# Where the two halves of the weights begin in a partition: 192 and 64 modulo 256 in place of 128

## The reference, cut to what matters

```
h = rms_norm(x, norm_mix_w);  z = h @ w_in + b_in            # 1024 x 5640
mixed = sigmoid(..) * (ya @ w_proj_att) + sigmoid(..) * (yb @ w_proj_mlstm)
x = x + mixed @ w_out
h2 = rms_norm(x, norm_mlp_w)
x = x + square(relu(h2 @ w_ff1)) @ w_ff2                     # 1024 x 4096, 4096 x 1024
```

## Time and profile before

| | |
|---|---|
| time, median of 3 runs | 2530.49 us (2530.07 to 2531.1) |
| profiled execution: its time, its span | 2530.58 us, 2528.8 us |
| PE busy | 2458.0 us, 97% of the span |
| PEld busy | 1994.5 us, 79% |
| POOL, DVE, ACT busy | 1098.9, 991.2, 870.1 us |
| DMA | 215.18 MB, 85 GB/s on average |
| granted TensorE clock | 0.991 on average |

### The profile page before, as it was taken

The page is one execution under the profiler, slowest core; times in us unless marked ns, Lnnn a source line. Parts: engine busy times, 40 slices in busy tenths (PEclk is TensorE's granted clock), DMA queues, the critical chain, the costliest instruction groups (busy, mean ns, idle before and its releaser), DMA issues.

```text
span 2528.8 us, 30042 instructions
## 1 busy us (share of the span) xinstructions
PE 2458.0 (97%) x11732; PEld 1994.5 (79%) x11732; DVE 991.2 (39%) x1582; ACT 870.1 (34%) x1093; POOL 1098.9 (43%) x808
## 2 busy tenths in 40 slices
PE   8899999999999999899999999999999999999998
PEld 6767788888888867688888888798776688888887
DVE  4545564310212354564320212557585534322202
ACT  4255333331323345333431323442234323322213
POOL 4332345554544422335554554342343245555543
PEclk9999999999999999999999999999999999999999
DMA  4221223223322221223222322231122133223221
GB/s 138 84 67 51 67 84 100 86 98 100 100 100 88 84 67 51 79 71 100 83 100 100 100 99 69 84 92 51 52 88 67 55 100 100 89 93 100 100 100 67
DMA packets 174028, 215.18 MB, mean 85 GB/s; under 512 B 7652, under 2 KB 155044, under 8 KB 173924
## 3 DMA queue, kind: packets, MB, share of 16 engines
q1 hardware_dynamic: 171572, 210.39, 25.9%
q10 hardware_dynamic: 2352, 3.31, 0.4%
HBM read 211.20 MB, written 2.10 MB: 84 GB/s over the span
## 4 chain that ended last, share of the span: by engine, by line
issue 49%; POOL 30%; PE 19%; DMA 0%; POOLq 0%; DVE 0%; ACT 0%; SPq 0%
POOL w_lo L290 30%; PE ps L331 3%; PE ps L330 3%; PE ps L329 3%; PE ps L736 3%; PE ps L1755 2%; PE ps L1753 2%; PE ps L1757 2%; DMA w_raw<-in_w_in 0%; POOLq L301 0%; PE ps L322 0%; PE ps L355 0%; PE ps L349 0%; PE ps L348 0%; PE ps L319 0%
## 5 line engine op out<-in xcount | busy, mean ns | idle before, releaser
L290 POOL TENSOR_TENSOR w_lo<-w_raw,w_hi 128x512 fp32r<-128x512 f32 x804 | 1098.7, 1399 | 1403.2 <-ACT w_hi L276 1391.2
L276 ACT ACTIVATE w_hi<-w_raw 128x2048 fp32r<-128x2048 f32 x200 | 382.9, 1915 | 1033.0 <-PE ps L331 394.0
L736 PE MATMUL ps<-h_hi,w_hi 128*128 128x512 f32 (+1 forms) x936 | 393.8, 421 | 15.1 <-POOL w_lo L290 12.9
L736 PE MATMUL ps<-h_hi,w_lo 128*128 128x512 f32 (+1 forms) x936 | 369.0, 394 | 0.0
L736 PE MATMUL ps<-h_lo,w_hi 128*128 128x512 f32 (+1 forms) x936 | 368.5, 394 | 0.0
L329 PE MATMUL ps<-h_hi,w_hi 128*128 128x512 f32 x816 | 319.0, 391 | 0.0
L331 PE MATMUL ps<-h_hi,w_lo 128*128 128x512 f32 x816 | 317.5, 389 | 0.0
L330 PE MATMUL ps<-h_lo,w_hi 128*128 128x512 f32 x816 | 317.4, 389 | 0.0
L736 PEld LDWEIGHTS ps<-h_hi,w_hi 128*128 128x128 f32 (+1 forms) x936 | 175.8, 188 | 76.2 <-issue 23.1
L736 PEld LDWEIGHTS ps<-h_lo,w_hi 128*128 128x128 f32 (+1 forms) x936 | 175.6, 188 | 43.1 <-issue 7.5
L736 PEld LDWEIGHTS ps<-h_hi,w_lo 128*128 128x128 f32 (+1 forms) x936 | 175.2, 187 | 41.4
(11 more groups left out here) (408 smaller groups left out, 3665.6 us busy)
## 6 DMA issues: line engine op xcount, KB each, us to landing
w_raw<-in_w_in SPq DMA_DIRECT2D x72, 1024.0 KB, 5.2
w_raw<-in_w_ff SPq DMA_DIRECT2D x64, 1024.0 KB, 5.2
w_raw<-in_w_ffn_in SPq DMA_DIRECT2D x22, 1024.0 KB, 5.1
w_raw<-in_w_out SPq DMA_DIRECT2D x12, 1024.0 KB, 5.1
w_raw<-in_w_ffn_out SPq DMA_DIRECT2D x11, 1024.0 KB, 4.9
w_raw<-in_w_proj_att SPq DMA_DIRECT2D x4, 1024.0 KB, 5.0
w_raw<-in_w_proj_mlstm SPq DMA_DIRECT2D x4, 1024.0 KB, 5.1
w_raw<-in_w_up_ssd SPq DMA_DIRECT2D x4, 1024.0 KB, 5.3
```

Source lines behind the costliest of these rows:

```text
L276: act.activation(k.whi[:, slot * SLOT:(slot + 1) * SLOT], k.wraw[:, slot * SLOT:(slot + 1) * SLOT], ACT.Copy).then_inc(k.hi_done, CHUNKS)
L290: pool.tensor_tensor(k.wlo[:, a:a + T], k.wraw[:, a:a + T], k.whi[:, a:a + T], ALU.subtract)\
L736: mm = pe.matmul(out, lhs, rhs, start=i == 0 and n == 0, stop=stop and n == 2)
```

## The change

The bytes at which tensors begin are moved. `w_hi` lies 64 bytes further up, at 192 modulo 256. Another 128 bytes are left free ahead of `w_lo`, which so lies 192 bytes further up, at 64 modulo 256, and all that is placed behind it (`xT`, `w_raw`, `constants`, `cos`, `sin` and the small ones) moves up by 192 bytes as well. `h_hi`, `h_lo` and the arena stay where they are. Every engine has the same instructions in the same order as before.

```diff
         k.arena, k.arena_words = (k.top + 127) // 128 * 128, ARENA
         k.top = k.arena + 4 * ARENA
-        k.whi, k.wlo = k.keep("w_hi", 2 * SLOT, F32R), k.keep("w_lo", 2 * SLOT, F32R)
+        k.top += 64
+        k.whi = k.keep("w_hi", 2 * SLOT, F32R)
+        k.top += 128
+        k.wlo = k.keep("w_lo", 2 * SLOT, F32R)
         k.xT = k.keep("xT", KD * T)
         k.wraw = k.keep("w_raw", 2 * SLOT)
```

## The result

The changed kernel takes 2565.65 us (median of 4 runs, 2565.2 to 2566.81), the kernel before, run beside it, 2530.28 us (median of 4, 2529.84 to 2531.1). The ratio is **1.014, with a 95% interval of 1.0123 to 1.0158**: 35.4 us slower. I had predicted 2530.5 us, no change that can be told. The prediction was wrong, and the time lies outside its range (2506 to 2550) as well.

The account below looks back on a forecast made before the run. The prediction took the kernel as bound by how fast PE can start matmuls (226.7 ns each). All terms were 0, so the profiled 2530.58 us, 0.1 us above the median, gave 2530.5 us; range 2506 to 2550 us.

Parts of the forecast that it names:

- Loaded pieces move against the stream: 8952 matmuls loading weights beside streamed tokens: moved load starts cost 0 us, bounds -119 to +49 us.
- Seven of the eight possible offsets, one spacing: Job loading 8 columns, stepping 32 bytes per tile: triples claimed at 0.69, 0.695 and 0.693 us whatever the load's start.
- the readings meet more: Slower rival, loads and streams on PE: 2550 or 2569 us; chance 0.06 from 2550 us, 0.08 for 2536 to 2550.
- the narrow jobs: Jobs loading only 8 or 16 columns on PE: 0.693 us a triple, claimed unchanged wherever the load starts.
- The rule weighed in the prediction: PE's separate SBUF read ports: loading the next tile takes nothing from the running matmul, so the change is worth 0 us.
- ACT and POOL at other offsets: ACT and POOL access `w_raw`, `w_hi`, `w_lo` at new offsets: 0 us; +6 or -6 us if POOL changed 10%.
- DMAs further up: Weight loads landing 192 bytes further up: 0 us, hidden, 5.2 us in a unit of 10.9.
- The streamed weights: 1248 matmuls in which weights stream, from moved starts: 0 us, bounds +-17 us.
- the extra: 13.3 ns per reduced-float32 matmul at full clock, above one column per tick (213.3 ns for 512 columns).
- The bound of +49 us: Upper bound for 8952 moved loads on PE: stream never settles, +5.5 ns each.
- faster: Rival: load and stream readings part; 2395 us if wholly (chance 0.07), 2506 to 2525 us in part (0.11).

Follow-up runs that it names:

- e1_behind: Only what lies behind `w_hi` and `w_lo` moved 192 bytes further up against the kernel before: 2530.81 us, ratio 1.0003.
- e3_all64: Weights, streamed activations and arena all moved 64 bytes further up against the kernel before: 2529.85 us, ratio 1.0002.
- e13_alone: Kernel before plus an appended stage of matmuls, PE alone, start of load minus start of stream chosen per line: 226.7 ns at 0, 233.3 at 64 bytes.
- e11_both224: Both `w_hi` and `w_lo` moved 224 bytes further up against the kernel before: 2576.7 us, ratio 1.018.
- the alternations: Lines of e13_alone in which two pairs of load and stream starts alternate: 228.5, 230.0, 232.1 and 233.3 ns.

## Why the prediction was wrong, step by step

**The step that failed** is "Loaded pieces move against the stream", which I costed at "0 ns x 8952 = 0 us". It measured +5.2 ns in the settled stretches (226.6 to 231.8) and +39.2 us over the 8715 matmuls that pay it. Nothing else of the change costs: e1_behind, with the weights at their old places and only what lies behind them moved, is at 1.0003, and e3_all64, where weights and streams move together, at 1.0002. Two thoughts led to the 0, and both are wrong:

- From the earlier trace rows, 8 and 16 columns at one spacing whatever their start, I concluded for all loads. They speak for narrow loads alone. And the earlier trace rows left out the triple ahead of them, the only one of the job at distance 0, which took 0.68 us in place of 0.693: the sentence "Seven of the eight possible offsets, one spacing" stood on six offsets that were timed, and the two that were missing held the one that differs. e13_alone shows both side by side: 8 columns 231.0 and 231.8 ns at distance 0 and 64, 128 columns 226.7 and 233.3.
- "A load of 128 columns passes over 512 bytes, twice around 256, and would meet every slice whatever its start." Its start matters all the same, 226.7 against 233.3 ns. It passes every slice, but at a time that its start sets against the stream; the loads with wider steps, which lose the 226.7 at distance 0, speak for that, though no run shows the two readings in time. The load of one word is at 229.2, 231.8 and 231.8; so the wide load doesn't only disturb. At distance 0 it helps by 2.5 ns against a load of one word and 4.3 against one of 8 columns, at 64 it costs 1.5.

The sentence "That narrow loads run at 693 / 3 = 231 ns although they read far fewer bytes than wide ones at 226.7 speaks once more against a meeting of the two readings" read a true sign the wrong way round. It was the sign that 226.7 is a special state which wide loads reach and narrow ones don't. The rival "the readings meet more" said so ("a lucky one into which the stream settles") and gave 2569 us, 3 us from what came; I gave it 0.06 from 2550 us on, against 0.64 for no change. Its direction was right and the number near by luck: it took 4.3 ns each where the settled stretches show 5.2, counted 8952 where 8715 pay and many pay less, and the stream doesn't settle where narrow loads keep it, since with all loads at 64 it goes on to 233.4. Its argument was the only one in the text that explained and the narrow jobs together, and it deserved a larger share.

**The rule weighed in the prediction.** The Trainium skill ("TensorE: Matmul & The Clock Gate", Part 2) says that loading the next tile takes nothing from the running matmul, through a read port of its own. For reduced float32 the runs here don't bear out what I took from it, that the load's start can't matter: it alone moves the spacing from 226.7 to 233.3 ns. The 215.8 ns that follow from the page's gap for 512 columns are not reached here either; the nearest is 217.7 to 218.5 ns, for a stream that stays within 32 bytes.

**Right:** what bounds the kernel (PE's starts; in all ten kernels that move tensors the time went with the spacing). *ACT and POOL at other offsets* and *DMAs further up* at 0: e1_behind, 1.0003. *The streamed weights* near 0: 120 to 117.8 ns, -4.8 us of the -17 to +17 allowed; the reason given, that turning the roles changes nothing, was wrong (e13_alone: distance 64 is the faster one there). That the extra sits in full-clock reduced float32 alone: half clock and plain float32 didn't move. The bound of +49 us held as a number (e11_both224, with every load at a bad distance, +46), and the range should have reached that far; its two factors were off against each other, 6.8 ns measured where 5.5 were allowed (226.6 to 233.4), on fewer matmuls at that pace than 8952. The rival *faster* falls: of all distances tried with 128 columns loaded and 512 streamed, 0 is the best.

**Open.** Whether the 8 to 15 ns above 218.5 are a collision with the load's reading or a cost of the stream's own change from slice to slice: every matmul has a load beside it, and the load of one word doesn't take it away, which speaks for the latter; it wasn't separated further. Why walks of 16 and 32 words cost more than the whole tile. Why 4 bytes of distance already lose the good state, why 192 costs so little when both halves have it, and why the alternations come out as they do: measured, not explained.

## What to carry to other kernels

Where matmuls of reduced float32 with 128 columns loaded and 512 streamed follow one another without a gap, keep the loaded piece and the streamed tile at the same place modulo 256 bytes: it was worth up to 1.8% of this kernel (1.4% in the change itself), and any allocator that packs tensors by size can lose it without a changed instruction. Other shapes want their own test: with 256 columns streamed a distance of 64 was better than 0, with 64 loaded 128 was about as good. Compare the time between starts with another kernel's, not busy shares, since PE read 97% busy in both. When a trace shows one spacing for one shape and another for the next (231 and 226.7 ns here), ask what makes the faster one fast before costing an edit at nothing by the slower one. And when rows serve as a test of an idea, see that the case you stand in (here distance 0) is among them.

## What the runs showed of the hardware that I had not expected

- The start of a load changes the pace of the stream beside it: 226.7 ns at distance 0 modulo 256, 229 at 192, 233.3 at 32, 64 and 224, for 512 columns of reduced float32 at full clock (2.4 GHz). At half clock (426.7 ns in both kernels) and with plain float32 (17.33 us a line at distance 0 and 64) it changes nothing.
- A wide load can make the stream faster than a narrow one does: 226.7 against 231.0 ns.
- With 256 columns streamed the order turns: 121.0 ns at distance 0, 117.9 at 64.
- A stream within 32 bytes runs at 217.7 to 218.5 ns, within 64 bytes at 242 to 247, the slowest of all, and from 256 bytes on at 227 to 233. The Trainium skill ("SBUF — State Buffer", Specifications) has lines of 16 bytes, where each crossing to a new one pays. Here a walk over two such lines (8 words) paid nothing, and the cost began at 64 bytes.
